# A decoder trunk of two layers: the projections begin with four of the twelve conditioning pieces, and the activations keep one function table

## What is computed

```python
'w_ada': nrm((DEPTH, D_MODEL, 6 * D_MODEL), 0.5 * D_MODEL ** -0.5),
'b_ada': nrm((DEPTH, 6 * D_MODEL), 0.05),
...
def rms_norm(x, gain):
    xf = x.astype(jnp.float32)
    y = xf * lax.rsqrt(jnp.mean(xf * xf, axis=-1, keepdims=True) + NORM_EPS)
    return y.astype(x.dtype) * gain
```

## Time and profile before

| | us |
|---|---|
| median of 3 runs | 2121.47 |
| lowest, highest | 2120.15, 2121.56 |
| the profiled execution | 2124.86 |
| its span, first to last instruction | 2123.1 |
| granted clock of TensorE over the span | 0.886 of full |

### The profile page before, as it was taken

How to read it: one execution, slowest core, us unless ns; L and a number is a source line. 1 busy time by engine, 2 the same in 40 slices (tenths; PEclk the granted TensorE clock), 3 DMA queues, 4 the chain that set the end, 5 groups by cost and what they waited for, 6 DMA issues and landing times.

```text
span 2123.1 us, 21282 instructions
## 1 busy us (share of the span) xinstructions
PE 1721.5 (81%) x8685; PEld 971.1 (46%) x8685; DVE 823.0 (39%) x1193; ACT 466.3 (22%) x612; POOL 297.0 (14%) x305
## 2 busy tenths in 40 slices
PE   2387786958777969999999679987459699999984
PEld 2243554437665464444444335564334544444432
DVE  3914677146552132322222235543540323223224
ACT  2021221244441111111111033433421201111103
POOL 6059848000000000000000100000000000000000
PEclk9688898979888959999999879978679599999996
DMA  7864432120001167999998231111001679999922
GB/s 262 306 210 147 139 112 86 40 80 3 3 3 41 68 239 275 325 322 330 325 321 314 99 119 60 40 40 40 0 0 49 249 267 334 325 320 327 325 84 103
DMA packets 162790, 357.37 MB, mean 168 GB/s; under 512 B 6825, under 2 KB 33693, under 8 KB 162717
## 3 DMA queue, kind: packets, MB, share of 16 engines
q1 hardware_dynamic: 144832, 297.90, 40.5%
q10 hardware_dynamic: 10396, 31.16, 3.7%
q0 software_dynamic: 7488, 27.27, 3.4%
HBM read 328.00 MB, written 28.31 MB: 168 GB/s over the span
## 4 chain that ended last, share of the span: by engine, by line
PE 62%; DVE 20%; ACT 10%; POOL 3%; DMA 2%; issue 2%; POOLq 0%; DVEq 0%; ACTq 0%; SPq 0%
PE banks L1342 11%; PE banks L1325 11%; PE banks L1329 11%; DVE work L1402 8%; PE banks L1274 5%; PE banks L952 5%; DVE small L1408 2%; PE banks L923 2%; PE banks L941 2%; PE banks L978 2%; PE banks L1314 2%; DVE work L1571 1%; DVE work L1408 1%; DVE x_features L1408 1%; DMA y_features<-in_w_ada_dram 1%
## 5 line engine op out<-in xcount | busy, mean ns | idle before, releaser
L952 PE MATMUL banks<-h_features,ring 128*128 128x512 f32 (+1 forms) x656 | 299.8, 613 | 12.9 <-ACT h_features L673 6.3
L1405 DVE TENSOR_SCALAR work<-work 128x512 f32<-128x512 f32 (+6 forms) x66 | 26.8, 405 | 568.4 <-ACT work L856 503.0
L578 POOL COPY idx_cur<-idx_tok 128x1 int32 (+1 forms) x36 | 6.6, 182 | 1499.6 <-DVE idx_tok L1980 881.3
L952 PEld LDWEIGHTS banks<-h_features,ring 128*128 128x128 f32 (+1 forms) x656 | 124.6, 194 | 165.9 <-issue 156.3
L1402 DVE TENSOR_TENSOR work<-work 128x512 f32<-128x512 f32 (+9 forms) x193 | 150.2, 778 | 16.5 <-ACT work L811 4.9
L1325 PE MATMUL banks<-ring,work 128*128 128x512 f32 x272 | 125.8, 618 | 2.4 <-ACT work L846 2.4
L1342 PE MATMUL banks<-work 128*128 128x512 f32 x272 | 120.8, 597 | 5.9 <-DVE work L2003 5.9
L1342 PE MATMUL banks<-ring,work 128*128 128x512 f32 x272 | 120.8, 597 | 5.9 <-DVE work L2003 5.9
L1274 PE MATMUL banks<-y_features,ring 128*128 128x512 f32 x256 | 114.4, 610 | 12.4 <-DVE small L1875 12.4
L1325 PE MATMUL banks<-work 128*128 128x512 f32 x272 | 119.5, 592 | 0.0
L1329 PE MATMUL banks<-work 128*128 128x512 f32 x272 | 119.5, 592 | 0.0
(11 more groups left out here) (338 smaller groups left out, 2331.9 us busy)
## 6 DMA issues: line engine op xcount, KB each, us to landing
ring<-in_w_gate_dram SPq DMA_DIRECT2D x17, 2048.0 KB, 8.4
ring<-in_w_up_dram SPq DMA_DIRECT2D x17, 2048.0 KB, 10.1
ring<-in_w_down_dram SPq DMA_DIRECT2D x17, 2048.0 KB, 9.7
work<-in_w_gate_dram SPq DMA_DIRECT2D x17, 2048.0 KB, 8.5
work<-in_w_up_dram SPq DMA_DIRECT2D x17, 2048.0 KB, 9.8
work<-in_w_down_dram SPq DMA_DIRECT2D x17, 2048.0 KB, 9.7
ring<-in_w_ada_dram SPq DMA_DIRECT2D x12, 2048.0 KB, 8.4
y_features<-in_w_ada_dram SPq DMA_DIRECT2D x24, 1024.0 KB, 5.2
```

What stands on the lines that cost most here:

```text
L952: ins = mm(PS[0:w, b, :], lhsT=W[:, k, c0:c0 + w], rhs=h[:, k, :], start=(k == 0), stop=(k == KD - 1))
```

## The change

Six things are changed, all of them in the code of layer 0's start and projections, except the last.

1. `chunk_plan()`: four ada pieces lie ahead of the projection pieces, and pieces 4 to 7 alternate with these. Pieces 8 and 9 go to a place of their own ("early"), the first 4096 columns of work, free once x is turned. Columns of pieces 10 and 11 become four more halves (`GATE_HALVES`), so POOL has 28.
2. DVE multiplies pieces 0, 1 and 3 ahead of the projections (`first_modulation` then needs 16 columns), and pieces 4, 8, 5, 9, 6, 7 behind its copies of blocks 1, 2, 4, 5, 8 and 11 (`ADA_AFTER`). It adds in place, in the ring. PE's sums of them stand behind blocks 2, 4, 6, 7, 9 and 13 (`ADA_SUMS_AFTER`).
3. Piece 2 is multiplied on PE (`ada_row`): eight products with cond as the weights give a row of 512, ACT copies it, and four products with a single one turn it into columns.
4. The halves' sums stand behind blocks 5 to 26 (`halves_after`), and SP's order of ring loads and halves is written out (`RING_ORDER`, `HALVES_BY`). A slot is free when PE has summed the piece, not when DVE has read it.
5. Four small parameter loads and the waits for POOL's constants and the parameters are moved behind the norm or into the projections; the parameter rows are turned ahead of the pieces.
6. ACT loads the table `natural_log_exp_and_others` at its start and once more behind the tanh.

```diff
+    plan = [("ada", 0, i) for i in range(4)]
+    for i in range(4):
+        plan += [("in", 0, i), ("ada", 0, 4 + i)]
+    plan += [("in", 0, i) for i in range(4, 7)]
+
+    plan += [None, None] + [("out", 0, i) for i in range(2)]
...
+        ADA_ORDER = [0, 1, 2, 3, 4, 8, 5, 9, 6, 7]
+        ADA_AFTER = {1: 4, 2: 5, 4: 6, 5: 7, 8: 8, 11: 9}
+        ADA_SUMS_AFTER = {2: 4, 4: 5, 6: 6, 7: 7, 9: 8, 13: 9}
+        turned_row = acc[0:1, 0, :]
+        early = work[:, 0:4096].rearrange("p (k n) -> p k n", n=512)
...
+        GATE_HALVES = 4
+        HALVES = 24 + GATE_HALVES
+        HALVES_BY = {5: 2, 6: 3, 8: 5, 7: 6, 10: 8, 9: 10, 12: 11, 11: 15, 13: 17, 14: 28}
+        RING_ORDER = [0, 1, 2, 3, 4, 5, 6, 8, 7, 10, 9, 12, 11, 13, 14]
...
+        def halves_after(n):
+
+            return [i for i in range(HALVES) if 5 + 7 * i // 9 == n]
...
                     if kind == "ada":
-                        sp.wait_ge(sem("ada_used"), 12 * l + i + 1)
+                        sp.wait_ge(sem("ada_summed"), ADA_ORDER.index(i) + 1)
...
+            for n in RING_ORDER:
+                load(n)
+                if n == 5:
+                    load_early(8)
+                if n == 7:
+                    load_early(9)
+                while halves_loaded < HALVES_BY.get(n, 0):
+                    load_half(halves_loaded)
+                    halves_loaded += 1
...
-            pool.wait_ge(sem("ada_summed"), 12)
...
+            act.preload_act_table_set("natural_log_exp_and_others")
             act.dma_start(work[0:KD, 4096 + 2 * P:4096 + 3 * P], A["c"][0].rearrange("(k p) -> k p", p=P)).then_inc(sem("c_loaded"), 16)
...
+                if n == 0:
+                    late_parameters()
+                    act.wait_ge(sem("row_summed"), 1)
+                    act.activation(turned_row, PS[0:1, 3, :], ACT.Copy).then_inc(sem("row_copied"), 1)
                 if n < 4:
-                    act.wait_ge(sem("amul_ready"), l + 1)
+                    act.wait_ge(sem("amul_ready"), 2 if n else 1)
...
                         link(act.activation(wad[0:64, :], wad[0:64, :], ACT.Tanh))
+                        act.preload_act_table_set("natural_log_exp_and_others")
...
+            def ada_row(n):
+
+                pe.wait_ge(sem("setup_step"), 1)
+                arrived(pe, ("ada", 0, n))
+                pe.wait_ge(sem("x_copied"), KD)
+                w = ring_ap(("ada", 0, n))
+                for k in range(KD):
+                    ins = mm(PS[0:1, 3, :], lhsT=cond[:, k:k + 1], rhs=w[:, k, :], start=(k == 0), stop=(k == KD - 1))
+                ins.then_inc(sem("row_summed"), 1)
+                pe.wait_ge(sem("row_copied"), 1)
+                for j in range(4):
+                    ins = mm(PS[:, 7, 4 * n + j:4 * n + j + 1], lhsT=turned_row[:, j * P:(j + 1) * P],
+                             rhs=ones[0:1, 0:1], start=True, stop=True)
+                ins.then_inc(sem("ada_summed"), 1)
...
-                    if l == 0 and 1 <= n <= HALVES:
-                        half_sums(n - 1)
+                    if l == 0:
+                        if n in ADA_SUMS_AFTER:
+                            ada_sums(ADA_SUMS_AFTER[n])
+                        for i in halves_after(n):
+                            half_sums(i)
...
-            for i in range(12):
-                ada_chunk(i)
-                if i == 5:
-                    norm(0)
-                if i == 9:
-                    parameters()
-                    lower_bounds()
-            dve.wait_ge(sem("pool_const"), 2)
-            modulation(0)
+            ada_chunk(0)
+            parameters()
+            ada_chunk(1)
+            norm(0)
+            ada_chunk(3)
+            first_modulation()
+            lower_bounds()
             projections(0)
-            modulation(1)
+            other_modulation()
```

More of the change, by code:

```diff
@@ L423, in load_half, with load_early @@
                     sp.wait_ge(sem("half_used"), i - 1)
-                sp.dma_start(half_place[i % 2], A["w_ada"][1].rearrange("(k p) n -> p k n", p=P)
-                             [:, :, 256 * i:256 * (i + 1)]).then_inc(sem(f"half_loaded{i % 2}"), 16)
+                l, c = half_layer(i)
+                sp.dma_start(half_place[i % 2], A["w_ada"][l].rearrange("(k p) n -> p k n", p=P)
+                             [:, :, c:c + 256]).then_inc(sem(f"half_loaded{i % 2}"), 16)
+            def load_early(i):
+                if i == 8:
+                    sp.wait_ge(sem("x_turned"), KD + 1)
+                else:
+                    sp.wait_ge(sem("ada_summed"), ADA_ORDER.index(8) + 1)
+                sp.dma_start(early, A["w_ada"][0].rearrange("(k p) n -> p k n", p=P)
+                             [:, :, i * 512:(i + 1) * 512]).then_inc(sem("early_loaded"), 16)
             def load(n):
@@ L455, in _ @@
                         load(n)
[L456 to L461, removed]
                     n += 1
@@ L1192, in rwkv @@
             def rwkv():
+                pe.wait_ge(sem("pool_const"), 2)
                 pe.wait_ge(sem("yhalf"), 1)
@@ L1353, in experts @@
                     ins.then_inc(sem("comb_turned"), 1)
-            pe.wait_ge(sem("pool_const"), 2)
-            pe.wait_ge(sem("params_loaded"), 16 * 9)
-            for i in range(12):
-                if i == 4:
-                    norm(0)
-                if i == 8:
-                    pe.wait_ge(sem("rows_loaded"), 16 * (len(ROWS1) + len(ROWS2)))
-                    n1 = sum(n for _, n in ROWS1)
-                    tr(PS[:, 4, 0:n1], work[0:n1, 4096:4096 + P], ident[0:n1, 0:n1])
-                    tr(PS[:, 4, P:2 * P], work[:, 4096 + P:4096 + 2 * P], ident).then_inc(sem("x_turned"), 1)
-                ada_sums(i)
+            pe.wait_ge(sem("rows_loaded"), 16 * (len(ROWS1) + len(ROWS2)))
+            n1 = sum(n for _, n in ROWS1)
+            tr(PS[:, 4, 0:n1], work[0:n1, 4096:4096 + P], ident[0:n1, 0:n1])
+            tr(PS[:, 4, P:2 * P], work[:, 4096 + P:4096 + 2 * P], ident).then_inc(sem("x_turned"), 1)
+            ada_sums(0)
+            norm(0)
+            ada_sums(1)
+            ada_row(2)
+            ada_sums(3)
             projections(0)
@@ L1420, in _, with ada_chunk @@
             signal(tt(cond, cexp, PS[:, 5, 0:KD], ALU.mult), "setup_step")
-            def ada_chunk(i):
-                arrived(dve, ("ada", 0, i))
-                if i >= 2:
-                    dve.wait_ge(sem("ada_summed"), i - 1)
-                w = ring_ap(("ada", 0, i))
-                a = acc[:, i % 2, :]
-                link(tsc(a, w[:, 0, :], cond[:, 0:1], ALU.mult))
+            def ada_chunk(n):
+                i = ADA_ORDER[n]
+                if i >= 8:
+                    dve.wait_ge(sem("early_loaded"), 16 * (i - 7))
+                else:
+                    arrived(dve, ("ada", 0, i))
+                w = ada_weights(i)
+                a = w[:, 0, :]
+                link(tsc(a, a, cond[:, 0:1], ALU.mult))
                 for k in range(1, KD - 1):
@@ L1511, in projections @@
                         signal(ins, "proj_copied")
+                    if l == 0 and n in ADA_AFTER:
+                        ada_chunk(ADA_AFTER[n])
+                    if l == 0 and n == 0:
+                        late_parameters()
                     for step in steps_after(l, n):
```

69 lines of the change are left out of this document (41 added, 28 removed).

## The result

| | before | changed |
|---|---|---|
| median, us | 2121.51 | 2038.49 |
| lowest, highest | 2120.15, 2127.92 | 2035.89, 2039.78 |
| span of the profiled execution | 2123.1 | 2038.0 |
| granted clock over the span | 0.886 | 0.898 |

The ratio is 0.9601, with a 95% interval of 0.958 to 0.9623: 83 us faster, where 75.3 were forecast (2046.2). The time lies in the range, but two of the forecast's terms are off by more than that suggests, in opposite directions.

What follows compares the result with a forecast made beforehand. TensorE carried 62% of the path, DVE 20%, ACT 10%. An earlier rwkv start (26.3 us) plus the function table (49.0) gave 75.3 off 2124.86, so 2049.6; less 3.4 for the median, 2046.2, range 2012 to 2070.

Steps and rivals of the forecast that it cites:

- The start: Before layer 0's projections: with four pieces ahead, one on PE, they start at 47.8 instead of 116.13, 68.3 us gained.
- The pieces beside POOL: Layer 0's projections: a DVE piece beside two POOL halves takes 19 to 20 us, not 6.0; piece 9 runs alone.
- What is given back: Layer 0's projections lose 17.1, 12.9, 14.3 and 0.3 us, regain 1.6 and 1.0; rwkv starts 26.3 earlier.
- the term of 12.9: Ahead of layer 0's first scores: piece 6 10.4 us, its sums and a half's 1.8, DVE's copy 0.7.
- The table in rwkv: Fewer loads at rwkv's front, in three inversions and at its end save 21.5 us, counted as waits alone.
- The table elsewhere: Behind rwkv: four norms 5.1 us, layer 1's projections, convolution blocks and gated steps 19.9, end of the ssd part 2.5.
- No sharing: Layer 0: pieces don't share in turn with POOL and cost 6.0 us each; time 2007.5 us, chance 0.13.
- All 61 loads count: Whole chain: all its table loads count, 78.3 us instead of 55; time 2023 us, chance 0.10.
- Half the loads: Behind rwkv's start: removed loads uncover PE or DVE waits, half of 49 us remains; time 2071, chance 0.11.
- the table not kept: On ACT: an activation of another set in between brings the loads back; time 2101 us, chance 0.03.
- 2.6 us a switch: On the path: ACT's draining makes each of 43 loads that count cost 1.3 us more; time 1990, chance 0.02.
- the SP queue as the limit: Layer 0: loading and POOL's work don't overlap, a half takes 15.7 us; slower, 2163 us, chance 0.03.

Runs made afterwards that it cites:

- the extra products: The kernel before, with 12 and 8 extra PE products in the two places of rwkv's tiles 0 to 2 where PE waits for ACT: 2110.69 us, 0.993.
- the loads put back: The changed kernel with four table loads put back into rwkv for each of tiles 1 to 3: 2058.64 us, 0.9681.
- the table alone: The kernel before with the shared function table only (two preloads, nothing else moved): 2059.45 us, 0.9701.
- the three rows: The changed kernel with pieces 9, 6 and 7 also multiplied on PE as rows, behind blocks 7, 8 and 13: 1998.26 us, 0.9414.
- a fourth: The kernel with three more rows on PE, and piece 4 as a row too, behind block 2: 2009.65 us, 0.9465.
- A start 5.8 us later: The changed kernel with piece 2 multiplied on DVE again instead of as a row on PE: 2040.24 us, 0.9608.

## Why the prediction was right, and where it was not

**The start.** Forecast 68.3 us, measured 72.0. Every step came in its order: the turns ended at 19.65 (23 forecast), the norm's products at 28.2 (33), piece 3 at 41.05 (45.3), the first projection at 44.15. Each of PE's steps was 3 to 5 us early. The row was hidden, as said (8.72 us of products from 30.54, its nearest row 8.86).

**The pieces beside POOL.** Forecast 16.5, 17.6, 19.9, 6.0, 10.4 and 20 us for pieces 4, 8, 5, 9, 6 and 7. Measured, with the first instruction: 16.4, 11.6, 11.2, 16.1, 8.4 and 15.7. The mechanism is the one of the earlier trace rows; the sizes scatter, because a piece pays for the POOL instructions that it happens to meet. Piece 9 met them after all, 10.1 us more than forecast: the step that had it alone failed, and pieces 8 and 5, 14.7 us shorter than forecast, hid that.

**What is given back.** To the alpha products 20.6 us (forecast 17.1), to the first scores 16.9 (12.9), to level 2's merge 10.2 (14.3), from there to rwkv 2.0 lost where 2.3 were to come back: 49.7 in all against 42.0. The first 3.5 us of the miss: the alpha products came at 127.70, as forecast (127.8), though the projections had begun 3.7 us earlier than forecast. Of the next 4.0, the alpha products and the block behind them, at 3.75 and 9.93 us instead of 2.25 and 8.52, are 2.9: PE was slower behind its wait of 15.95. The decay sums, left unchanged, are 2.1 (24.8 us instead of 22.7), and the term of 12.9 itself was 11.8. I priced what was moved, and not how it changes PE's speed and the steps that stay. The level products are no part of it: here are their first two groups in the changed kernel, and then the first of the kernel before, whose second took 14.71:

```profile
187.94 10.73 DVE L1473 TENSOR_TENSOR work<-work 64x256 f32<-64x256 f32 x7
205.30 15.26 DVE L1473 TENSOR_TENSOR work<-work 64x256 f32<-64x256 f32 x7
```

```profile
221.89 10.64 DVE L1402 TENSOR_TENSOR work<-work 64x256 f32<-64x256 f32 x7
```

All seven groups take 64.9 us in place of 68.4. Piece 7 was 4.3 us shorter than forecast, which matches the gain at level 2's merge; where the 4.3 us of the tail went stays open.

**The table in rwkv.** Forecast 21.5 us (the terms named there add up to 20.9), measured 31.6, and here the step failed that counted a load as a wait and no more. It sized the first wait of a tile rightly (2.55 us of 2.57) and took 0.6 too much for the second (1.66 of 2.27), where a wait of 1.22 is left; and it left PE's speed as it was. The granted clock was the missing term: 0.84 before, 0.93 after, 10.5 us by the extra products and 3 to 10 by the loads put back. A further part is scatter: with the table alone the stretch gained 26.8 us, not 31.6, and with the same rwkv code it took 260.73 us here, 264.20, 264.25, 265.55 and 265.72 in four other kernels, and 272.9 and 273.6 in two more, one profiled execution each.

**The table elsewhere.** Layer 1 from its projections to norm 3: 22.7 against 19.9 + 2.5. The layer-1 limit that the chain doesn't show was read rightly from PE's 98% in the earlier trace rows. The remaining norms and experts gave 8.5 instead of 5.1.

**Rivals.** No sharing (2007.5): false, by the rows of the pieces. All 61 loads count (2023): not so, though the table was worth 58.7 us (alone) to 62.8 (in the changed kernel) behind rwkv's start, between 49 and the 72 of this rival (49 and its 23 more). Half the loads (2071), the table not kept, 2.6 us a switch, the SP queue as the limit: none seen. The point of 46 to 52 us for the first projection was missed by 2 us on the fast side.

So the total is right within 8 us because layer 0 gave back 7.7 us more, the start came 3.7 earlier, and the part behind rwkv's start brought 13.8 more. That these nearly cancel is luck: the mechanisms named were the right ones, but the clock was missing from both sides, as a loss in layer 0 (2.9 us up to the first scores) and as a gain in rwkv.

## What to carry to other kernels

Where DVE and POOL both work on SBUF operands, cost a moved DVE step by what it will run beside, and expect that the steps left in place change too; a step of PE in its own idle time is cheaper, as the three rows show (40 us), though a fourth cost 11. A short ACT instruction between PE's products can cost its length and then PE's clock for the next products, so read the granted clock behind each wait before pricing it away. Split a change into its parts on the chip: here two preloads brought 3.0 of 4.0%.

## What was not expected of the hardware

- Extra products that fill PE's idle time made the kernel before 15 us faster; the clock of 20 us stretches behind waits of 4.2 and 2.9 us had been 0.70 to 0.91. With waits of 1.6 and 1.2 us most of them were 1.00.
- A start 5.8 us later cost nothing 370 us on, by which of POOL's instructions DVE met; and a fourth row, after which DVE met a half that POOL had begun 0.3 us before it, made the kernel 11 us slower instead of faster.
